# Token lists of all expert blocks built once by indirect 4-byte stores; gathers and weight loads four blocks ahead

## The chip, the cores and the metric

The kernel runs on one core of a Trainium2 chip. The metric is the device time of one launch in microseconds (us): 3921.82 us before, the median of three runs (3912.93, 3921.82 and 3946.88). TensorE (PE) multiplies matrices, and its weight loads are shown apart (PEld); VectorE is DVE, ScalarE is ACT, GpSimd is POOL and SyncE is SP. SP issues the plain loads on one DMA queue, POOL issues plain and indirect transfers on another; 16 DMA engines serve both.

## The reference, cut to what matters

Two layers of a diffusion backbone. Each mixes tokens (attention, pooling, windowed attention) and then runs a mixture of experts (MoE) over 768 tokens in layer 0 (256 context tokens and 512 latent ones) and over the 512 latent tokens in layer 1. A token chooses 8 of 64 experts. Each expert's tokens are padded to blocks of 128:

```python
idx = lax.top_k(sel, TOP_K)[1]                      # 8 experts of each token
order = jnp.argsort(flat_e)                         # assignments sorted by expert
dest = pad_start[sorted_e] + jnp.arange(A) - start[sorted_e]
row_tok = jnp.full((n_rows,), T, jnp.int32).at[dest].set(order // TOP_K)
...
def expert_block(args):                             # once per block of 128 rows
    tok, e = args
    xb = h_pad[tok]
    return (jax.nn.silu(xb @ w_eg[e]) * (xb @ w_eu[e])) @ w_ed[e]
...
routed = jnp.zeros((T + 1, D), h.dtype).at[row_tok].add(y * row_w[:, None])[:T]
return routed + shared                              # shared: one expert for all tokens
```

D_MODEL is 1024, an expert's hidden width 256, all of it in float32: the three weight matrices of a block are 1024 KB each. With the inputs of this case layer 0 has 76 blocks and layer 1 has 65, together 141.

## The kernel before, in words

All engines run programs written out by hand; a plan (`make_plan`, L74) lists jobs in one order that PE, ACT and DVE all follow, with three rotating PSUM slots: a job's PE part waits until the job three before it has been drained. Everything up to the MoE loop is such jobs. Those around the change, for each tile t of 128 tokens: `r` (router scores), `sg` (gate and up projection of the shared expert, L1000), `sT` and `sd` (transpose and down projection, L1005 and L1013), `pos` (each token's number within its expert, by triangular matmuls, L1020), then once `cnt`, `end`, `tab` (the table of blocks: expert, and place within the expert), and `first`.

`route` (L1320) is DVE's choice of 8 experts for a tile; POOL then stores the tile's weights into `h_rows` in DRAM (L1753), behind the token's row of 1024 floats. The outputs of the shared expert go to `acc` in DRAM, on POOL's queue (L1756, L1781).

**The expert loop** (`moe`) handles one block per step. PE's order in step n: gate and up matmuls of block n (L747, 16 records), eight transposes of the gathered rows of block n+1 (L719), `slots_of` (L734: one-hot times token numbers gives the token list of block n+2), the down matmuls of block n-1 (L783, 8 records), two transposes of the hidden rows of block n. DVE makes the one-hot (L1372), turns the product into indices (`take_index`, L1379 to L1384), halves the copies out of PSUM with ACT (L1389, L1430, L1401) and multiplies gate by up (L1396). POOL gathers rows with an indirect DMA (L1765) and adds results into `acc` with another (L1774; even and odd blocks go to two accumulators, and each store waits until the one of its accumulator two blocks before it has landed). The index of block n+2 is kept in one of four columns; before it is written, DVE waits for the store of block n-2, which uses that column. There are two buffers for gathered rows and two for weights (`WSL`, K and VY). SP loads gate and up of block n+2 when the gate and up matmuls of block n are done, and down of block n+1 when the down matmuls of block n-1 are done.

After the loop all engines meet, and `combine` adds the accumulators to the residual stream.

## Time and profile before

| what | value |
|---|---|
| median of the runs | 3921.82 us |
| the profiled execution's own time | 3961.87 us |
| its span, first to last instruction | 3960.0 us |
| mean granted PE clock | 0.930 of full speed |
| busy: PE, PEld, DVE, ACT, POOL | 91%, 56%, 30%, 19%, 13% |
| expert loop, layer 0 | from about 1218 to 2229 us |
| expert loop, layer 1 | from about 3059 to 3913 us |
| weight loads per block | 3 of 1024 KB |

The two expert loops are nearly half of the span. In a row of the timeline the columns are: start, duration, engine, line, operation, output and input tile, shapes, count; in brackets the idle time before it and what ended it. A row of the windows gives busy time of each engine with its number of instructions, then the granted clock, the busy share of the 16 DMA engines and the rate in GB/s.

### The profile page before, as it was taken

The page shows a single profiled execution, that of the slowest core. Times are in us where ns is not written, and L with a number is a line of the kernel's source. Part 1 is how long each engine was busy: PE and PEld are TensorE (multiplying, and loading weights), DVE is VectorE, ACT ScalarE, POOL GpSimd, SP SyncE. Part 2 cuts the span into 40 slices and gives each one's busy share as a digit, 9 for nine tenths or more (in the row PEclk, how much of TensorE's full clock was granted, in tenths as well). Part 3 has the DMA queues.
Part 4 walks back from the last instruction along what each step waited for, and adds up shares of the span by engine and source line. Part 5 has one row for each costly group of instructions (what it writes and reads, how often), then busy time and mean ns, then how long its engine had stood idle before and what let it go on. Part 6 is the DMA issues. An engine that isn't in the chain of part 4 may idle for free.

```text
span 3960.0 us, 45512 instructions
## 1 busy us (share of the span) xinstructions
PE 3595.2 (91%) x14248; PEld 2233.7 (56%) x14248; DVE 1173.0 (30%) x2319; ACT 756.3 (19%) x1339; POOL 518.1 (13%) x418
## 2 busy tenths in 40 slices
PE   7899999999998998999999499999998999999994
PEld 3479777799654444444444247876764444444442
DVE  2252222123242222222222425333323222222223
ACT  2342222121111111111111225232211111111111
POOL 0000300000001121222222300010000112122122
PEclk9999856999998999999999799979998999999997
DMA  6310100343327999999999720102323999999996
GB/s 225 97 33 27 62 22 16 113 148 114 128 87 259 305 294 293 296 317 301 309 318 297 227 79 1 46 17 64 96 98 146 301 302 293 304 309 302 294 300 187
DMA packets 221226, 735.22 MB, mean 186 GB/s; under 512 B 45573, under 2 KB 93863, under 8 KB 166980
## 3 DMA queue, kind: packets, MB, share of 16 engines
q1 hardware_dynamic: 174420, 596.12, 41.8%
q0 software_dynamic: 46704, 137.66, 15.3%
q8 instruction: 74, 1.21, 0.1%
q14 instruction: 28, 0.23, 0.0%
HBM read 671.68 MB, written 97.88 MB: 194 GB/s over the span
## 4 chain that ended last, share of the span: by engine, by line
PE 62%; DMA 26%; DVE 5%; issue 4%; ACT 1%; POOLq 1%; SPq 0%; DVEq 0%; POOL 0%; ACTq 0%
DMA acc<-region_q,idx 14%; DMA region_c<-h_rows,idx 12%; PE ps L783 8%; PE ps L719 7%; PE ps L690 6%; PE ps L890 6%; PE ps L697 5%; PE ps L699 5%; PE ps L698 5%; PE ps L909 5%; PE ps L747 5%; PE ps L983 3%; PE ps L1000 2%; PE ps L811 1%; DVE region_q L1430 1%
## 5 line engine op out<-in xcount | busy, mean ns | idle before, releaser
L719 PEld LDWEIGHTS ps<-con,region_c 128*128 128x128 f32 x2342 | 333.6, 183 | 390.3 <-DMA region_c<-h_rows,idx 202.1
L719 PE MATMUL ps<-con,region_c 128*128 128x128 f32 x2342 | 393.8, 305 | 167.5 <-DMA region_c<-h_rows,idx 141.2
L747 PE MATMUL ps<-region_k,region_q 128*128 128x512 f32 x1136 | 502.4, 595 | 1.7 <-DVE region_q L1389 1.7
L747 PE MATMUL ps<-region_v,region_q 128*128 128x512 f32 x1120 | 492.4, 592 | 0.8 <-DVE region_q L1389 0.8
L1050 ACT ACTIVATE region_q<-ps 128x512 f32<-128x512 f32 (+2 forms) x310 | 195.3, 630 | 837.0 <-PE ps L783 483.7
L747 PEld LDWEIGHTS ps<-region_k,region_q 128*128 128x128 f32 x1136 | 211.9, 192 | 241.7 <-issue 241.7
L747 PEld LDWEIGHTS ps<-region_v,region_q 128*128 128x128 f32 x1120 | 207.9, 191 | 235.4 <-issue 234.4
L1765 POOL DMA_INDIRECT region_c<-h_rows,idx x145 | 152.0, 1048 | 1301.6 <-DVE idx L1384 1104.9
L699 PE MATMUL ps<-region_x_split,ring_split 128*128 128x384 f32 (+2 forms) x800 | 284.9, 356 | 0.0
L783 PE MATMUL ps<-region_k,region_c 128*128 128x512 f32 x568 | 283.2, 644 | 1.0 <-DVE region_c L1401 1.0
L783 PE MATMUL ps<-region_v,region_c 128*128 128x512 f32 x560 | 273.7, 634 | 1.0 <-DVE region_c L1401 1.0
L1396 DVE SCALAR_TENSOR_TENSOR region_c<-region_c,ps 128x256 f32<-128x256 f32 x141 | 67.8, 481 | 688.4 <-ACT region_c L1066 688.4
L1774 POOL DMA_INDIRECT acc<-region_q,idx x141 | 238.9, 1694 | 198.1 <-DVE region_q L1430 150.9
L1066 ACT ACTIVATE region_c<-ps 128x256 f32<-128x256 f32 x141 | 54.2, 384 | 910.8 <-PE ps L747 910.8
L783 PEld LDWEIGHTS ps<-region_k,region_c 128*128 128x128 f32 x568 | 111.0, 206 | 116.2 <-issue 116.2
L783 PEld LDWEIGHTS ps<-region_v,region_c 128*128 128x128 f32 x560 | 107.6, 203 | 111.0 <-issue 111.0
L697 PE MATMUL ps<-region_x_split,region_q_split 128*128 128x384 f32 (+1 forms) x432 | 159.0, 368 | 7.5 <-DVE ring_split L1312 4.6
L1372 DVE TENSOR_TENSOR region_c<-con,posm 128x768 bf16 (+1 forms) x147 | 123.1, 837 | 125.7 <-issue 125.7
L699 PEld LDWEIGHTS ps<-region_x_split,ring_split 128*128 128x128 f32 x800 | 152.4, 190 | 12.0
L1430 DVE COPY region_q<-ps 128x512 f32<-128x512 f32 x141 | 97.5, 692 | 207.6 <-PE ps L783 206.8
L1389 DVE COPY region_q<-ps 128x512 f32<-128x512 f32 x143 | 98.3, 688 | 191.7 <-PE ps L719 191.7
L698 PE MATMUL ps<-region_h_split,region_q_split 128*128 128x384 f32 (+1 forms) x432 | 153.6, 355 | 0.0
(268 smaller groups left out, 4490.4 us busy)
## 6 DMA issues: line engine op xcount, KB each, us to landing
region_k<-in_w_exp_gate SPq DMA_DIRECT2D x71, 1024.0 KB
region_k<-in_w_exp_up SPq DMA_DIRECT2D x71, 1024.0 KB
region_k<-in_w_exp_down SPq DMA_DIRECT2D x71, 1024.0 KB, 7.8
region_v<-in_w_exp_gate SPq DMA_DIRECT2D x70, 1024.0 KB
region_v<-in_w_exp_up SPq DMA_DIRECT2D x70, 1024.0 KB
region_v<-in_w_exp_down SPq DMA_DIRECT2D x70, 1024.0 KB, 8.1
ring<-in_w_mod SPq DMA_DIRECT2D x24, 2048.0 KB, 8.0
ring<-in_w_in SPq DMA_DIRECT2D x26, 1024.0 KB, 5.7
```

The source lines that it names most:

```text
L690: last = mm(ps[0:rows, at:at + n], weight[k], src[k][:, tok:tok + n], start=k == 0, stop=k == len(weight) - 1)
L697: mm(o, wh, xh, start=k == 0, stop=False)
L698: mm(o, wh, xl, start=False, stop=False)
L699: last = mm(o, wl, xh, start=False, stop=k == len(stationary) - 1)
L719: last = nc.tensor.transpose(ps[0:t.shape[1], at:at + t.shape[0]], t, ident[0:t.shape[0], 0:t.shape[0]])
L747: last = mm(m_gu[s], xgT[:, s, k, :], wgu[s][:, :, k, :], start=k == 0, stop=k == DK - 1)
L783: last = mm(m_y[:, 512 * side:512 * side + 512], hTb[:, 1 - s, cc * P:cc * P + P], wdn[1 - s][:, cc, 512 * side:512 * side + 512], start=c ...
L890: last = mm(ps[:, at:at + n], q, k, start=True, stop=True)
L909: last = mm(OB[g % 2][:, VD * h:VD * h + VD], PTb[:, i % 2, j * P:j * P + P], v, start=j == 0, stop=j == len(ks) - 1)
L1050: return A_(o, i, ACT.Copy)
L1765: pool.indirect_dma_start(xg[:, s, :], None, H, bass.IndirectOffsetOnAxis(ap=idx[:, i4:i4 + 1], axis=0), bounds_check=TOK - 1, oob_is_err= ...
L1774: pool.indirect_dma_start(ACC[s], bass.IndirectOffsetOnAxis(ap=idx[:, i4:i4 + 1], axis=0), yb[:, s, :], None, compute_op=ALU.add).then_inc ...
```

## The change

The one-hot products, `take_index` and the `first` job are gone. Instead, `place_tokens` computes for each tile and each of its 8 choices one address in a list in DRAM (`slot_list`, 128 x 384 numbers, a column for every possible block of every expert), and POOL stores the token numbers there with 8 indirect DMAs of 128 x 4 bytes per tile: 48 in layer 0, 32 in layer 1. The lists were filled with numbers of dummy tokens at the start of the kernel. SP then loads the whole list back into SBUF once (192 KB), DVE shifts it right by 3 bits, and in the loop POOL copies the column of a block into a small index tile before each gather and each adding store.

`pos` of a tile now follows its `sg` job, so the routes and the placing alternate with the shared expert's work; the last two come after the last but one `sg`. The stores of the shared expert's results move from POOL's queue to SP's. There are four buffers of gathered rows (two of them in `region_h`) and four of weights (two of them in the ring of weight panels). SP loads block n+4 when block n is done; POOL gathers block n+3 in the step in which block n-1 is added.

```diff
-            if i == len(A) - 1:
-                for u in A:
-                    add("pos", l, u, drain="dve")
+            add("sg", l, t, drain="dve", panel=("shgu", l))
+            if i < len(A) - 1:
+                add("pos", l, t, drain="dve")
+            if i == len(A) - 2:
+                add("pos", l, A[-1], drain="dve")
                 add("cnt", l, drain="dve")
                 add("end", l, drain="dve")
                 add("tab", l, drain="dve")
-                add("first", l)
-            add("sg", l, t, drain="dve", panel=("shgu", l))
...
-        WSL = [K, VY]
+        WSL = [K, VY, ring[:, 0:6144], ring[:, 6144:12288]]
...
+                sp.wait_ge(sl["listed"], 16 * TOPK * len(A))
+                sp.dma_start(slots, LISTS[l].rearrange("(p n) a -> p (n a)", p=P)).then_inc(sl["list_in"], 16)
+                for n in (len(A) - 2, len(A) - 1):
+                    store_shared(n)
+                sp.wait_ge(filled, names["sd", l, A[-1]].fill)
+                for n in range(2, DEPTH_W):
+                    load_gate_up(expert(n), n)
+                    load_down(expert(n), n)
...
-                            with sp.If(n + 2 < n_blocks):
+                            with sp.If(n + DEPTH_W < n_blocks):
+                                e = expert(n + DEPTH_W)
                                 sp.wait_ge(sl["gu_done"], n + 1)
-                                load_gate_up(expert(n + 2), s)
-                            with sp.If(n + 1 < n_blocks):
-                                sp.wait_ge(sl["dn_done"], n)
-                                load_down(expert(n + 1), 1 - s)
+                                load_gate_up(e, r)
+                                sp.wait_ge(sl["dn_done"], n + 1)
+                                load_down(e, r)
...
-                                pe.wait_ge(sl["idx_ready"], n + 2)
-                                slots_of(r + 1, n + 3)
...
+            def place_tokens(l, t, ps):
+                ...
+                stt(base, ps[:, 0:E], float(LISTN), cst("listbase"), ALU.mult, ALU.add)
+                link(tt(past, ps[:, 0:E].unsqueeze(2).broadcast_to([P, E, MAXB - 1]), levels, ALU.is_gt))
+                vec.tensor_reduce(b, past, AX.X, ALU.add).then_inc(drained["dve"], 1)
+                dve.wait_ge(drained["dve"], names["pos", l, t].count)
+                link(stt(u, b, 1.0 - P * LISTN, base, ALU.mult, ALU.add))
+                link(tt(u, u, M, ALU.mult))
+                link(vec.max(best[:], u))
+                ts(place[:, 8 * n:8 * n + 8], best[:], -1.0, None, ALU.add).then_inc(placed, 1)
...
+                dve.wait_ge(sl["list_in"], 16)
+                ts(slots, slots, 3, None, ALU.logical_shift_right).then_inc(sl["slots_ready"], 1)
...
-                                dve.wait_ge(sl[f"scat{s}"], 16 * (UNROLL // 2 * m + (r + 1) // 2 + 1))
-                                take_index(n + 3, (r + 3) % 4)
...
                     pool.wait_ge(w_ready, n + 1 + (NT if l else 0))
                     pool.dma_start(H[t * P:t * P + P, D:HROW], Wt[:, n % 2, :]).then_inc(s_w[n % 2], 16)
+                    pool.wait_ge(placed, n + 1 + (NT if l else 0))
+                    for j in range(TOPK):
+                        at = bass.IndirectOffsetOnAxis(ap=place[:, 8 * n + j:8 * n + j + 1], axis=0)
+                        pool.indirect_dma_start(LISTS[l], at, choices[:, 8 * t + j:8 * t + j + 1], None)\
+                            .then_inc(sl["listed"], 16)
...
+                def gather(w, n, free=None):
+                    at = column(n)
+                    if free is not None:
+                        pool.wait_ge(sl["h_ready"], free)
+                    gp.tensor_copy(idx_in[:, w:w + 1], slots[:, bass.ds(at, 1)]).then_inc(sl["in_ready"], 1)
+                    pool.wait_ge(sl["in_ready"], n + 1)
                     pool.sem_inc(turns, 1)
-                    pool.indirect_dma_start(xg[:, s, :], None, H, bass.IndirectOffsetOnAxis(ap=idx[:, i4:i4 + 1], axis=0),
-                                           bounds_check=TOK - 1, oob_is_err=False).then_inc(sl[f"gat{s}"], 16)
...
+                def add_block(s, k, before):
+                    at = column(k)
+                    pool.wait_ge(sl[f"scat{s}"], 16 * (before + 1))
+                    gp.tensor_copy(idx_out[:, s:s + 1], slots[:, bass.ds(at, 1)]).then_inc(sl["out_ready"], 1)
+                    pool.wait_ge(sl["out_ready"], k + 1)
                     pool.wait_ge(sl["y_a"], k + 2)
                     pool.wait_ge(sl["y_b"], k + 2)
...
-                            with pool.If(n < n_blocks):
-                                pool.wait_ge(sl["h_ready"], n + 1)
-                                gather(s, (r + 3) % 4, n + 3)
+                            with pool.If(n + 3 < n_blocks):
+                                gather(r, n + 3, n)
```

## Rows read from the trace of the kernel before

**Rows 1.** Windows: the two expert loops, an undisturbed 48 us, and 5 us after a wait.
```profile
1218.00:2229.00 1011.00, 933.31 (x3040) 466.42 (x3040) 281.16 (x609) 120.04 (x229) 209.97 (x153) 0.96 0.92 296
3059.00:3913.00 854.00, 785.46 (x2470) 389.75 (x2470) 222.70 (x521) 102.45 (x196) 175.51 (x131) 0.97 0.92 293
...
2020.00:2068.00 48.00, 45.40 (x157) 22.59 (x156) 14.14 (x32) 6.32 (x12) 10.42 (x8) 1.00 1.01 335
...
1465.00:1470.00 5.00, 5.00 (x16) 2.64 (x15) 1.29 (x4) 0.60 (x1) 0.43 (x1) 0.50 0.73 305
```

**Rows 2.** One line's instructions (L747), then timelines at the loops' starts and ends.
```profile
L747 PE MATMUL ps<-region_k,region_q x1136: 592/592/1193, 1218.3 to 3902.4; 128*128 128x512 f32 x190
...
2228.42 0.69 DVE L1430 COPY region_q<-ps 128x512 f32<-128x512 f32 x1 [2.21 <-PE ps L783]
...
3059.26 7.11 PE L747 MATMUL ps<-region_k,region_q 128*128 128x512 f32 x16 [0.87 <-DVE region_q L1389]
...
3912.62 0.69 DVE L1430 COPY region_q<-ps 128x512 f32<-128x512 f32 x1 [2.28 <-PE ps L783]
```

**Rows 3.** Timeline of PE in layer 0's loop: a late step, then a prompt one.
```profile
1453.68 7.03 PE L747 MATMUL ps<-region_k,region_q 128*128 128x512 f32 x16
1463.90 1.97 PE L719 MATMUL ps<-con,region_c 128*128 128x128 f32 x8 [3.19 <-DMA region_c<-h_rows,idx]
...
1471.69 7.03 PE L747 MATMUL ps<-region_v,region_q 128*128 128x512 f32 x16
...
1479.45 0.29 PE L734 MATMUL ps<-tokb,region_c 128*128 128x3 bf16 x6
1479.60 3.68 PE L783 MATMUL ps<-region_k,region_c 128*128 128x512 f32 x8
...
1483.34 7.03 PE L747 MATMUL ps<-region_k,region_q 128*128 128x512 f32 x16
```

**Rows 4.** Waits of the whole span: total us, times, longest.
```profile
POOL region_c L1765 <- DVE idx L1384: 1104.9, 122, 12.3
...
PEld ps L719 <- DMA region_c<-h_rows,idx: 202.1, 75, 4.3
...
DVE pcol L1379 <- DMA acc<-region_q,idx: 169.8, 120, 3.0
```

**Rows 5.** Timeline in layer 0's loop: from an adding store to the gather behind it.
```profile
1702.20 2.32 POOL L1774 DMA_INDIRECT acc<-region_q,idx  x1 [0.30 <-issue]
...
1711.96 0.16 DVE L1379 COPY pcol<-ps 128x3 f32<-128x3 f32 x1 [0.98 <-DMA acc<-region_q,idx]
...
1713.48 1.04 POOL L1765 DMA_INDIRECT region_c<-h_rows,idx  x1 [8.96 <-DVE idx L1384]
...
1721.17 1.16 PE L719 MATMUL ps<-con,region_c 128*128 128x128 f32 x8 [0.15 <-DMA region_c<-h_rows,idx]
```

**Rows 6.** The adding stores (L1774), from issue to landing.
```profile
DMA to landing us min/median/max: 6.0/9.0/12.4
```

**Rows 7.** DMA issues, last figure us to landing: a 256 KB load, the expert-weight stores.
```profile
ring<-in_w_pool SPq DMA_DIRECT2D x2, 256.0 KB, 2.9
...
h_rows<-rt POOLq DMA_DIRECT2D x10, 32.0 KB, 1.7
```

**Rows 8.** Timeline ahead of the two loops, up to their first transposes.
```profile
1130.77 13.95 PE L1000 MATMUL ps<-ring,region_h 128*128 128x512 f32 x32
...
1138.47 0.54 POOL L1753 DMA_DIRECT2D h_rows<-rt  x1 [4.53 <-DVE rt L1357]
...
1183.32 0.19 PE L1020 MATMUL ps<-Mb,trib 128*128 128x64 bf16 x1
...
1216.24 1.16 PE L719 MATMUL ps<-con,region_c 128*128 128x128 f32 x8 [1.97 <-ACT region_q L1050]
...
2994.36 16.38 PE L1000 MATMUL ps<-ring,region_h 128*128 128x512 f32 x32
...
3057.24 1.15 PE L719 MATMUL ps<-con,region_c 128*128 128x128 f32 x8 [1.97 <-ACT region_q L1050]
```

More of the change, by code:

```diff
@@ L36 @@
 UNROLL = 4
+DEPTH_W = 4
+LISTN = E * MAXB
 HROW = D + E
@@ L44 @@
 _at = 0
-for _name, _n in (("ident", 128), ("ones", 128), ("perm16", 128), ("perm8", 128), ("tri", 128), ("tokid", 3 * NT), ("sel2", 2),
-                  ("thr", MAXB), ("iotan", TABN), ("dummy", 1), ("negdummy", 1), ("edges", 64), ("lower", 64),
-                  ("slot1", TOK)):
+for _name, _n in (("ident", 128), ("ones", 128), ("perm16", 128), ("perm8", 128), ("tri", 128), ("sel2", 2),
+                  ("thr", MAXB), ("iotan", TABN), ("edges", 64), ("lower", 64), ("listbase", E)):
     CONSTS[_name] = (_at, _at + _n)
@@ L262, in build @@
         scores = sb("scores", NT * E)
-        posm = sb("posm", NT * E)
+        key = sb("key", 3 * E)
+        over = sb("over", E * (MAXB - 1))
+        best = sb("best", 8)
+        place = sb("place", NT * 8, I32)
+        choices = sb("choices", NT * 8, I32)
         rt = sb("rt", 6 * E)
@@ L602, in _ @@
             for l in range(DEPTH):
+                sp.dma_start(LISTS[l].rearrange("(p n) a -> p (n a)", p=P), nobody).then_inc(s_empty, 16)
+            for l in range(DEPTH):
                 A = active(l)
@@ L620, in _, with store_shared @@
                 sl = L[l]
+                def store_shared(n):
+                    after(sp, "sd", l, A[n])
+                    sp.dma_start(ACC[0][A[n] * P:A[n] * P + P, :], yb[:, n % 2, :]).then_inc(s_sh[n % 2], 16)
                 sp.wait_ge(filled, names["o", l, A[-1]].fill)
+                for n in range(len(A) - 2):
+                    store_shared(n)
                 sp.wait_ge(tab_ready, l + 1)
@@ L722, in _, with moe @@
             tiles_done = [0]
-            def moe(l, part):
+            def moe(l):
                 sl = L[l]
@@ L746, in gate_up @@
                     for k in range(DK):
-                        last = mm(m_gu[s], xgT[:, s, k, :], wgu[s][:, :, k, :], start=k == 0, stop=k == DK - 1)
+                        last = mm(m_gu[s], xgT[:, s, k, :], wgu[w][:, :, k, :], start=k == 0, stop=k == DK - 1)
                     last.then_inc(sl["gu_done"], 1)
@@ L753, in turn_hidden @@
                     turn(m_h, [(cc * P, hv[:, cc, :]) for cc in range(2)]).then_inc(sl["hT_done"], 1)
-                if part == "first":
-                    slots_of(0, 1)
-                    pe.wait_ge(sl["idx_ready"], 1)
-                    slots_of(1, 2)
-                    return
                 turn_tokens(0, 16)
@@ L763, in moe @@
                 turn_tokens(1, 16)
-                slots_of(2, 3)
                 turn_hidden(0, 0)
@@ L1357, in route @@
                 ts(Wt[:, n % 2, :], t3, inv, ROUTED, ALU.mult, ALU.mult).then_inc(w_ready, 1)
-            def moe(l, part):
+            def place_tokens(l, t, ps):
+                M, (base, u, b) = Mb[:, t * E:t * E + E], (key[:, i * E:i * E + E] for i in range(3))
+                n = active(l).index(t)
+                a, _ = CONSTS["thr"]
+                levels = con[:, a + 1:a + MAXB].unsqueeze(1).broadcast_to([P, E, MAXB - 1])
+                past = over[:].rearrange("p (e k) -> p e k", e=E)
+                stt(base, ps[:, 0:E], float(LISTN), cst("listbase"), ALU.mult, ALU.add)
[6 more added lines that the diff above has]
+                ts(place[:, 8 * n:8 * n + 8], best[:], -1.0, None, ALU.add).then_inc(placed, 1)
@@ L1642, in _ @@
                     last = tt(hb[:, n % 2, :], s1[:, n % 2, :], ps[:, DE:2 * DE], ALU.mult)
-                    last.then_inc(drained["dve"], 1)
-                    last = None
-                    if n < 2:
-                        route(l, NT - 2 + n)
                 elif kind == "pos":
-                    t = a[1]
-                    last = tt(posm[:, t * E:t * E + E], ps[:, 0:E], Mb[:, t * E:t * E + E], ALU.mult)
+                    place_tokens(l, a[1], ps)
+                    n = active(l).index(a[1])
+                    if n + 2 < len(active(l)):
+                        route(l, active(l)[n + 2])
                 elif kind == "cnt":
@@ L1775, in add_block @@
                                             yb[:, s, :], None, compute_op=ALU.add).then_inc(sl[f"scat{s}"], 16)
-                for s in range(2):
-                    gather(s, s, s + 1)
-                for n in (len(A) - 2, len(A) - 1):
-                    after(pool, "sd", l, A[n])
-                    pool.dma_start(ACC[0][A[n] * P:A[n] * P + P, :], yb[:, n % 2, :]).then_inc(s_sh[n % 2], 16)
+                pool.wait_ge(sl["slots_ready"], 1)
+                for w in range(2):
+                    gather(w, w)
@@ L1782, in _ @@
+                pool.wait_ge(filled, names["sd", l, A[-1]].fill)
+                for w in range(2, UNROLL):
+                    gather(w, w)
                 for s in range(2):
```

148 lines of the change are left out of this document (55 added, 93 removed).

## The prediction

> **What bounds the kernel now.** I read the windows of the two expert loops first. They take 1011 and 854 us, and in both PE is busy 92% of the time, at 0.96 of its clock, with the DMA engines 92% busy at 296 and 293 GB/s [rows 1]. Nothing is idle enough to be ignored, so the bound must be read from single steps. The loops run from the first gate-and-up matmul at 1218.3 to the last copy's end at 2229.1, and from 3059.3 to 3913.3 [rows 2]: 1010.8 and 854.0 us, 1864.8 us for 76 and 65 blocks, a mean step of 13.23 us.
>
> PE's timeline shows that there is no typical step. From 1471.69 to 1483.34 one takes 11.65 us: the matmuls follow each other without a gap. The one before, from 1453.68, takes 18.01 us [rows 3]. After its gate-and-up matmuls PE waits 3.19 us for gathered rows, and after that pause its clock is granted at 0.50, the lower of its two levels (1.2 GHz), for the next 5 us [rows 1], so that the transposes take 1.97 us and the down matmuls are slow too. PE's weight loads wait for gathers 75 times, 202.1 us in all [rows 4]: about every second step is late. No comparable wait for weights is in the list.
>
> Why is the gather late? An adding store starts on POOL at 1702.20; DVE's `take_index` waits until it has landed, to 1711.96; the gather that it feeds is issued at 1713.48, and PE gets the rows at 1721.17 [rows 5]. So each gather stands behind the landing of a store four blocks older, because they share an index column. That is 19 us from store to rows, of which the step offers 18.5 (11.65 + 6.87 to the end of the next gate-and-up). DVE stands in that wait 120 times, POOL waits for the index 1104.9 us in total [rows 4]. The loop is held by this chain, with PE close behind and the DMA engines next.
>
> **What is removed.** (a) The chain goes: the lists exist before the loop. A gather in the new kernel is issued when block n-1 has been handed to its adding store and is used three blocks later; from the code, PE needs it some 19 us (one step and a gate-and-up part) after its issue even in steps of 11.65 us, against the 7.7 us of the one above [rows 5]. (b) PE loses `slots_of`, 0.15 us a step (the next matmul starts 0.15 us after its start at 1479.45 [rows 3]). So PE alone would need 11.5 us a step, 141 x 11.5 = 1621 us. (c) DVE loses one-hot, copy and index work; it is 28% busy in the loop [rows 1], so this pays nothing by itself.
>
> **What the loop then waits for.** The DMA engines carry 296 GB/s x 1011 us / 76 = 3.94 MB a block in layer 0 and 293 x 854 / 65 = 3.85 MB in layer 1, and the change leaves that as it is. At 11.5 us a step they would need 342 and 335 GB/s. Two readings bound what they can do. The best long stretch, four prompt steps, holds 335 GB/s at a share of 1.01 [rows 1]: 11.8 and 11.5 us a block. Taking instead the loop's share for real occupancy, 0.92 of 13.3 and 13.14 us gives 12.2 and 12.1 us. I take 12.0 us, nearer the second, because a 48 us stretch can live on weights that came early, the whole loop cannot: 141 x 12.0 = 1692 us, **-173 us**. Ends: 1621 (-243, PE alone) and 141 x 12.2 = 1720 (-145).
>
> The Trainium skill, "DMA: Bandwidth & Descriptors", section Specifications, puts the HBM limit of a core at about 358 GB/s. By that figure a block would take 11.0 us of transfers, PE would be the bound, and the loops would come to 1621 us. No stretch here holds such a rate for 48 us, so I let the row decide.
>
> Weights four ahead add no speed by themselves, as they are not late now; they only let DMA and PE drift apart by more.
>
> **What is added in the loop.** POOL gets two register loads and two copies of 128 x 1 a step. No row has them; from below zero, from above I allow 1 us each, 4 us on top of the 2.7 us of its two indirect issues (1.04 and 1.59 to 2.32 [rows 5]). POOL is then 7 us busy of 12, still covered. A new wait: `add_block` now stands on the landing of the store two blocks before it ahead of its copy, and the next gather is queued behind it on POOL. That landing takes 9.0 us, 12.4 at most [rows 6], two steps are 24 us, so it costs nothing while this cover lasts.
>
> **What is added ahead of the loops.** 80 indirect stores, each on POOL. The nearest row is a gather's issue, 1.04 us plus 0.3 of dispatch (1.34); the dearer one the adding store, 1.59 + 0.3 = 1.89 [rows 5]. A store without add is nearer the gather; I take 1.34. In layer 0 the first tile can be placed when `sg` of tile 0 is through: half of 13.95 after 1130.77 plus some 2.5 us for `pos` and placing, 1140 [rows 8]. From there POOL works through 48 x 1.34 + 6 x 0.84 (the weight stores) = 69 us, to about 1210; by the last two tiles alone, placed together near 1184, it would be 1184 + 16 x 1.34 = 1205. Then: the last store lands, 1.7 us [rows 7]; the list load of 192 KB, about 3 us like a 256 KB load [rows 7]; shift, register loads and copy, 2 us; gather, 1.04 issue and 7.2 landing beside 6 MB of weights [rows 5]. Sum 15 us: first rows at 1225, against 1216.24 now [rows 8]: +9 us. In layer 1, placing starts near 3004 (half of 16.38 after 2994.36, and pos [rows 8]), 32 x 1.34 + 3 gives 3050, rows at 3065 against 3057.24: +8. Together **+17 us**. At 1.89 the two are +35 and +26, **+61**. From below: PE no longer waits for the first lists between the `pos` jobs and the last `sg` (5 us), so if POOL keeps up each start is about 6 us earlier, **-12**.
>
> The Trainium skill says in the same page, section "Queues, rings and completion order", that the descriptors of one queue are taken in ring order on each engine. By that the list load, which SP issues behind two blocks of weights, waits for them; they are 6.3 MB from about 1190, 19 us at 335 GB/s, out by 1209 and so ahead of the list in any case. It matters only if POOL is faster than I think, and would cap the lower end at zero instead of -12.
>
> `place_tokens` and the route (5.07 us a tile [rows 8], placing some 2.5 by seven small operations) are 8 us of DVE in the 11.4 us that PE spends on a tile: nothing. The shared expert's stores on SP stand ahead of nothing that is due. The dummy lists (2 x 192 KB) and 24 KB of choices are loaded early, against 370 KB less of constants: nothing.
>
> **Sum.** -173 + 17 = -156 us. On the profiled execution's own 3961.9 that is 3806; on the median of 3921.8, which is 40 lower, 3766. Where those 40 us lie is not shown; if a part is gather waits that unprofiled runs don't have, the gain is a little smaller. **I say 3770.**
>
> **The rivals.**
> 1. PE becomes the bound, 11.5 us a step: -243 + 17 gives 3695. For it: the four prompt steps in a row at 335 GB/s. Against: the share is then already 1.01. 17%.
> 2. The DMA engines don't gain at all beyond their present mean and the start is dear: 12.4 us a step (1748, -117) and +61: 3866. For it: mixed stretches move fewer bytes. Against: the clean stretch. 16%.
> 3. The step stays where it is: gathers are still late, since POOL issues them in order behind an adding store that waits for y. Then +17: about 3939. Against: three blocks of lead. 6%.
> 4. Slower: the indirect transfers starve behind up to four blocks of weights. Place: the copy of y of block n waits for the landing of the store of n-2, so a step can't be shorter than (landing + 2.2)/2. It decides from a landing of 21.8 us and makes the kernel slower from 24.2. If three further blocks of weights, 9.4 MB, stood ahead, they alone would be 28 us; at a landing of 28 the step is 15.1 us, +264: about 4190. Against: with one to two blocks outstanding it is 9.0, never above 12.4 [rows 6]. The Trainium skill, same page and section, has each engine alternate between the queues packet by packet, which would double a landing at most, to 18 us: no cost. 8%.
>
> The forecast (11.7 to 12.3 us a step) has 53%.
>
> **The numbers.** Range 3690 to 3865: it takes in rival 1, the bound of +61 and most of rival 2. What a measurement can tell from no change is about 1%, 39 us. Faster by more: the forecast, rival 1 and nearly all of rival 2, 0.83. Within 1%: rival 3 and a rest, 0.08. Slower: 0.09.
>
> **What would show it.** Steps of 11.5 to 12.3 us; hardly a wait of L719 for `region_c<-h_rows`, short waits of L747 for weights instead if the DMA bound holds; a clock near 1.00 in the loop; DMA share 0.97 or more and 320 to 340 GB/s. The first transposes 9 us later than now in layer 0, and an issue of the small stores near 1.04 us. It is wrong if L1430 or L1050 wait for the adding store's landing, if POOL's busy time nears the step, or if the small stores take over 2 us each.

## The result, and the profile after

The kernel after takes **3712.2 us** (median of 4 runs, 3690.0 to 3785.4) against 3934.4 us for the kernel before (median of 4, 3912.9 to 3961.1): 0.941 of it, 95% interval 0.932 to 0.951. I had said 3770, range 3690 to 3865. The slowest of the four executions, 3785.4 us, was in a slower state; it counts in the median and not in the ratio. The profiled execution took 3699.5 us, its span 3697.7.

The page of the kernel after: busy time by engine, what the DMA engines moved in 40 slices of 92 us, and the chain that ended last.
```profile
PE 3436.1 (93%) x13496; PEld 2137.5 (58%) x13496; DVE 975.2 (26%) x1798; ACT 755.5 (20%) x1337; POOL 631.0 (17%) x767
...
GB/s 241 81 58 7 72 40 58 120 139 146 104 66 218 345 354 348 354 354 355 350 359 297 166 47 1 49 18 69 90 100 71 320 350 343 340 352 344 340 342 149
...
PE 90%; DVE 3%; DMA 2%; issue 1%; ACT 1%; POOL 1%; SPq 0%; another core or an unknown queue 0%; POOLq 0%; DVEq 0%; ACTq 0%
```
Nine tenths of the path is PE itself. The windows of the two loops and of 100 us inside the first (length; busy us and instructions of PE, PEld, DVE, ACT, POOL; granted clock, DMA share, GB/s), beside [rows 1]:
```profile
1178.00:2050.00 872.00, 869.77 (x2576) 431.84 (x2575) 159.18 (x303) 119.19 (x227) 226.43 (x295) 1.00 0.98 337
1600.00:1700.00 100.00, 100.00 (x301) 49.87 (x300) 18.83 (x36) 14.21 (x27) 27.63 (x36) 1.00 1.02 356
2903.00:3651.00 748.00, 745.21 (x2202) 369.91 (x2202) 136.45 (x260) 102.06 (x195) 192.22 (x251) 1.00 0.97 329
```
PE is busy for all but 2 us of 872, at full clock, and the DMA engines hold 356 GB/s for 100 us, where the stretch of before in [rows 1] has 335 for 48 us. By the first gate-and-up matmul and the last copy's end, as in [rows 2], the loops are 1177.7 to 2050.3 and 2903.3 to 3651.0: 872.6 and 747.7 us, 1620.3 in all against 1864.8, **-244.5 us**, and 11.48 and 11.50 us a step.

PE's timeline of one step, beside [rows 3]: no gap, no late gather.
```profile
1474.45 7.03 PE L765 MATMUL ps<-ring,region_q 128*128 128x512 f32 x16
1481.32 1.05 PE L743 MATMUL ps<-con,region_h 128*128 128x128 f32 x8
1482.21 3.60 PE L792 MATMUL ps<-region_v,region_c 128*128 128x512 f32 x8
1485.65 0.39 PE L743 MATMUL ps<-con,region_c 128*128 128x128 f32 x2
1485.87 7.03 PE L765 MATMUL ps<-ring,region_q 128*128 128x512 f32 x16
```
Waits of the whole span (total us, times, longest), beside [rows 4]:
```profile
POOL acc L1775 <- DVE region_q L1421: 1004.0, 134, 11.5
...
PE ps L743 <- DMA region_c<-h_rows,idx_in: 28.7, 2, 16.3
```
The 75 late gathers have become two, the first rows of each layer. POOL's 1004 us are its wait for y.

**Part of the difference is not the change.** In the stretch from 450 to 650 us, attention of layer 0, whose code is the same in both, the profiled execution of before had TensorE's clock granted at 0.55, the one of after at 0.97. A repeat of the kernel after (below) had 0.53. One window each of before, after and that repeat:
```profile
450.00:650.00 200.00, 197.47 (x719) 148.04 (x718) 53.85 (x136) 49.85 (x126) 11.63 (x12) 0.55 0.06 19
```
```profile
450.00:650.00 200.00, 190.27 (x1099) 147.24 (x1098) 70.00 (x164) 64.99 (x147) 16.97 (x19) 0.97 0.14 47
```
```profile
450.00:650.00 200.00, 196.93 (x696) 146.78 (x694) 52.55 (x135) 49.65 (x126) 14.51 (x18) 0.53 0.06 20
```
In the last column but two is the clock. With the stretch layer 0's router starts at 1120.1 (before) or 1134.4 (the repeat), without it at 1044.1. So the two profiles differ by 262 us, of which 76 lie there; 3961.9 against the repeat's 3776.9, both with it, gives **-185 us** at like clocks. Even there 14 us lie ahead of the router. They are clock too: run 1 below has the code of before up to the router and no low stretch, and its router starts at 1045.7, 1.6 us from the kernel after. So the change itself is nearer **-199 us**.

### The profile page after: what moved, and what is told of

Read it like the earlier page. It is cut to its first block, busy times and chain, and to the rows that moved or that the text cites. A ratio compares the mean times of both kernels' runs of the same rounds, so it can differ in the third digit from the quotient of the medians.

```text
span 3697.7 us, 42657 instructions
## 1 busy us (share of the span) xinstructions
PE 3436.1 (93%) x13496; PEld 2137.5 (58%) x13496; DVE 975.2 (26%) x1798; ACT 755.5 (20%) x1337; POOL 631.0 (17%) x767
## 4 chain that ended last, share of the span: by engine, by line
PE 90%; DVE 3%; DMA 2%; issue 1%; ACT 1%; POOL 1%; SPq 0%; another core or an unknown queue 0%; POOLq 0%; DVEq 0%; ACTq 0%
PE ps L765 26%; PE ps L792 13%; PE ps L743 8%; PE ps L714 7%; PE ps L721 5%; PE ps L722 5%; PE ps L723 5%; PE ps L899 5%; PE ps L918 4%; PE ps L992 4%; PE ps L820 1%; PE ps L1009 1%; POOL slot_list L1745 1%; PE ps L1004 1%; PE ps L876 1%
## 5 line engine op out<-in xcount | busy, mean ns | idle before, releaser
L765 PE MATMUL ps<-ring,region_q 128*128 128x512 f32 x1120 | 492.2, 592 | 0.0
L1775 POOL DMA_INDIRECT acc<-region_q,idx_out x141 | 226.3, 1605 | 1060.1 <-DVE region_q L1421 1004.0
L765 PEld LDWEIGHTS ps<-ring,region_q 128*128 128x128 f32 x1120 | 207.9, 191 | 234.4 <-issue 234.4
L743 PE MATMUL ps<-con,region_c 128*128 128x128 f32 x1766 | 281.0, 288 | 51.3 <-DMA region_c<-h_rows,idx_in 28.7
L765 PE MATMUL ps<-region_k,region_q 128*128 128x512 f32 x576 | 258.2, 602 | 1.7 <-DVE region_q L1389 1.7
L792 PE MATMUL ps<-ring,region_c 128*128 128x512 f32 x560 | 252.0, 593 | 1.0 <-DVE region_c L1401 1.0
L765 PE MATMUL ps<-region_v,region_q 128*128 128x512 f32 x560 | 246.3, 593 | 0.7 <-DVE region_q L1389 0.7
L765 PEld LDWEIGHTS ps<-region_k,region_q 128*128 128x128 f32 x576 | 108.8, 194 | 126.1 <-issue 126.1
L765 PEld LDWEIGHTS ps<-region_v,region_q 128*128 128x128 f32 x560 | 103.9, 191 | 118.2 <-issue 117.2
L792 PEld LDWEIGHTS ps<-ring,region_c 128*128 128x128 f32 x560 | 101.3, 191 | 102.6 <-issue 102.6
L992 PE MATMUL ps<-ring,region_k 128*128 128x512 f32 x320 | 138.7, 592 | 0.0
```

The source lines that it names most:

```text
L743: last = nc.tensor.transpose(ps[0:t.shape[1], at:at + t.shape[0]], t, ident[0:t.shape[0], 0:t.shape[0]])
L765: last = mm(m_gu[s], xgT[:, s, k, :], wgu[w][:, :, k, :], start=k == 0, stop=k == DK - 1)
L792: last = mm(m_y[:, 512 * side:512 * side + 512], hTb[:, 1 - s, cc * P:cc * P + P], wdn[before][:, cc, 512 * side:512 * side + 512], start= ...
L992: last = mm(ps[:, 512 * half:512 * half + 512], MG[:, k, t * P:t * P + P], w[:, k, :], start=k == 0, stop=k == DK - 1)
L1775: pool.indirect_dma_start(ACC[s], bass.IndirectOffsetOnAxis(ap=idx_out[:, s:s + 1], axis=0), yb[:, s, :], None, compute_op=ALU.add).then_i ...
```

## The experiments

"Start" below is the time from the first router matmul of a layer to the first gate-and-up matmul of its loop: 98.2 and 78.5 us before (layer 0, layer 1), 133.6 and 101.3 after. In layer 0 it also depends on the clock that the router got: with the router at the full clock, as before, the unchanged kernel after has 120.8 (run 11). Each run was timed against the kernel before on its own chip.

**1. Only the chain is cut, no lists.** The kernel before with eight index columns instead of four:
```
-UNROLL = 4
+UNROLL = 8
-        idx = sb("idx", 4, I32)
+        idx = sb("idx", 8, I32)
-                                dve.wait_ge(sl[f"scat{s}"], 16 * (UNROLL // 2 * m + (r + 1) // 2 + 1))
-                                take_index(n + 3, (r + 3) % 4)
+                                take_index(n + 3, (r + 3) % 8)
```


> The kernel before, with one thing changed: eight index columns instead of four (loop unrolled by eight), so that DVE need not wait for an adding store to land before it writes the next index. Gathers and weights keep their old depth. Theory A (the chain store landing -> index -> gather held the loop): the gather of block n+2 goes out when block n's hidden rows are read, 10 us before it is needed, against a landing of 7 to 8 us; the step falls from 13.2 to 11.7 to 12.0 us, the waits of PE for gathered rows from 202 us to under 40, the ratio to 0.94 to 0.955 (3690 to 3760 us). Theory B (gathers were late because of crowded DMA engines and shallow buffers): step 13.0 or more, ratio 0.985 to 1.0.

Measured: 3758.7 us, ratio 0.959 (0.943 to 0.974). Its loop of layer 0, and its waits:
```profile
1144.00:2078.00 934.00, 902.66 (x3040) 446.00 (x3040) 276.24 (x609) 120.03 (x229) 200.75 (x153) 1.00 0.98 320
```
```profile
PEld ps L719 <- DMA region_c<-h_rows,idx: 130.7, 111, 2.6
```
Steps of 12.29 and 12.11 us, loops of 1720.7: 144 of the 244 us come from the one wait for the store's landing, read from [rows 5]. The gathers are still late, by a little: 111 times, 1.2 us on the mean. So theory A has the cause, but its step of 11.7 to 12.0 us and its waits under 40 us were too good. The other 100 us came only with the lists, which take the index work out from between DVE, PE and POOL. That is by elimination, since neither depth alone is worth much (runs 2 and 3); the lists with both depths at two were not run.

**2 and 3. Depth.** The kernel after with two weight buffers instead of four, and with two buffers of gathered rows instead of four (the gather of block n+2 goes out when block n is hidden):
```
-        WSL = [K, VY, ring[:, 0:6144], ring[:, 6144:12288]]
+        WSL = [K, VY]
```


> The changed kernel with two weight buffers instead of four, loaded at the times of the kernel before. Theory A (depth of the weights adds nothing): step 11.5 us as with four, ratio to the kernel before 0.935 to 0.95. Theory B (the deeper queue is what lets the DMA engines carry 350 GB/s): step 12.0 us or more, PE waits at the gate-and-up matmuls for weights, rate at most 335 GB/s, ratio 0.96 or more.

```
-                            with pool.If(n + 3 < n_blocks):
-                                gather(r, n + 3, n)
+                            with pool.If(n + 2 < n_blocks):
+                                gather(s, n + 2, n + 1, (r + 3) % 4)
```


> The changed kernel with two buffers of gathered rows instead of four: the gather of block n+2 goes out when block n's hidden rows have been read, as early as the kernel before could have. Lists and four weight buffers stay. Theory A (the lists alone pay): about 10 us from issue to need; step 11.5 to 11.7 us if a landing takes 8 us, ratio 0.935 to 0.95. Theory B (beside weights queued four deep a landing takes longer than 10 us, so the lead is needed): PE waits 1 to 3 us for rows in many steps, step 12.5 to 13.5, ratio 0.97 to 1.0.

Measured: 3740.0 us (0.950, 0.935 to 0.965), steps 11.56 and 11.66; and 3708.0 us (0.946, 0.930 to 0.961), steps 11.50 and 11.51. Going four deep with weights is worth 0.1 us a step, some 16 us; with rows, about nothing (loops of 1622.2 against 1620.3). Once the lists exist, a gather has time enough from two buffers.

**4. How much the DMA engines carry.** Half of the down matmuls are left out (of each block only half of the output columns are computed), so that PE asks for weights faster:
```
-                                for side in range(2):
+                                for side in range(1):
```


> The changed kernel without the down matmuls of the second half of the output columns (4 of 8 records a step; all transfers stay). PE then needs 9.8 us a step. By the prediction's term (the DMA engines need 12.0 us a block) the step could not fall below 11.5 at all. If 350 GB/s at a share of 1.02 is their limit, the step is 11.0 to 11.2 us (3.9 MB at 352 GB/s) and PE waits for weights; if they still had room, it falls towards 9.8 us at up to 400 GB/s.

Measured: one run, 3687.8 us. Windows of layer 0's loop, of 100 us of it and of layer 1's loop, and the waits:
```profile
1168.50:2013.30 844.80, 770.21 (x2272) 384.21 (x2272) 159.41 (x303) 119.30 (x227) 226.63 (x295) 0.97 0.99 349
...
1650.00:1750.00 100.00, 93.42 (x281) 46.95 (x280) 20.03 (x38) 15.13 (x29) 27.66 (x36) 0.97 1.02 363
...
2889.10:3638.60 749.50, 694.29 (x2032) 345.67 (x2032) 142.58 (x271) 106.67 (x203) 201.57 (x263) 0.96 0.98 342
```
```profile
PE ps L765 <- DMA ring<-in_w_exp_up: 63.9, 40, 3.2
PE ps L765 <- DMA region_k<-in_w_exp_up: 33.1, 18, 3.2
```
Now PE does wait for weights, and the step of layer 0 stops at 11.12 us, though its matmuls alone need 9.8: that is about the transfers' own bound, 0.4 us under PE's. Layer 1 has 68 blocks here and not 65, because the halved sums of layer 0 change what its tokens choose. Its loop of 749.5 us is then 11.02 a step, at 342 GB/s. My 12.0 us a block was not the DMA engines' limit.

**5. The start doubled.** Every small store is done twice, the second to a list that nobody reads:
```
                             .then_inc(sl["listed"], 16)
+                    for j in range(TOPK):
+                        at = bass.IndirectOffsetOnAxis(ap=place[:, 8 * n + j:8 * n + j + 1], axis=0)
+                        pool.indirect_dma_start(SPARE[l], at, choices[:, 8 * t + j:8 * t + j + 1], None)\
+                            .then_inc(sl["listed"], 16)
```


> The kernel after with every small store done twice: behind a tile's 8 stores of 4 bytes a token stand 8 more of the same, to a second list that nobody reads, and the list load waits for all 160. It measures what a small store costs where it stands. At 1.26 us each (0.96 busy and 0.30 between) 48 more are 60 us of POOL in layer 0 and 32 more 40 us in layer 1. Theory A (POOL's stores are the path that sets the start of the loops only at the last two tiles, whose lists are made together): only the 16 added ones of these and what POOL falls behind before count, 20 to 45 us in layer 0 and 20 to 35 in layer 1, 40 to 80 us for the kernel. Theory B (POOL works through the stores without a pause, as my prediction had it): all 80 count, +100 us. Theory C (the stores are covered and the start waits for weights and the list's load): under +20 us. The loops keep 11.5 us a step in all three. If PE's and DVE's jobs ahead of the loops wait longer for each other too, the small stores disturb them (delays of 5 to 7 us that the kernel after shows at 1100 and 2850).

Measured: 3884.7 us (3816.1 to 3891.3). Starts 199.4 and 149.4: 65.8 and 48.1 us more, 113.9 in all, for 80 x 1.26 = 101 us of POOL. Theory B: POOL's stores are the path, from the first list to the last, and nearly every one counts. Not quite all of the burst is stores: in the kernel after POOL also waits 4.20 and 4.56 us for the placing of a tile in layer 0 and 4.07 in layer 1, and 8.52 in layer 0 here. Of the 13 us above the 101, 5.5 are the list, which lands 10.6 and 13.9 us after its issue against 8.9 and 10.1. The next two are the longest waits of PE in layer 0 and 1 without a release:
```profile
PE ps L1023 <- issue: 18.0, 1, 18.0
...
PE ps L1037 <- issue: 24.6, 1, 24.6
```

**6. The same number of plain stores.** The added ones are without indices:
```
+                    for j in range(TOPK):
+                        at = (8 * n + j) * P
+                        pool.dma_start(SPARE[l][at:at + P, :], choices[:, 8 * t + j:8 * t + j + 1]).then_inc(sl["listed"], 16)
```


> As the kernel with every small store doubled, but the added 8 a tile are plain stores of 4 bytes from each of 128 partitions, issued by POOL: the same number of packets of the same size, without indices. It asks what delays the other engines while POOL stores (DVE's chained operations 1.2 us apart instead of 0.26, a wait of PE of 18.0 us that no release explains). A plain store of Wt takes POOL 0.58 us, so 80 added ones are about 0.6 + 0.3 each, 70 us of POOL. Theory A (the 4-byte packets and their completions delay the others): the same delays, and the start longer by 70 to 80 us in all. Theory B (the making of indexed descriptors on POOL delays them): only POOL's own 70 us and no more delays than in the kernel after; +50 to +70 us. The loops stay at 11.5 us a step in both.

Measured: 3760.5 us (3739.8 to 3824.9); starts 152.4 and 126.4 against 120.8 and 101.6 of the control beside it (run 11), 56.4 us more for 80 x 0.55 = 44 us of POOL, as theory B had it. PE's unexplained waits in the starts are 1.8 and 5.8 us, against 4.6 and 8.8 in the control, so more packets of 4 bytes do not make them longer. But here DVE waits up to 14.5 us for the weight store (`Wt` has two buffers, and the store stands behind the small ones on POOL), and it does so too in run 5 (7.5 and 8.0 us): part of what looks like disturbance there is this wait. In both runs the starts grow by POOL's added time plus 12 to 13 us.

**7. The list on POOL's queue.** In the kernel after SP issues the list load behind two blocks of weights; here POOL does:
```
-                sp.wait_ge(sl["listed"], 16 * TOPK * len(A))
-                sp.dma_start(slots, LISTS[l].rearrange("(p n) a -> p (n a)", p=P)).then_inc(sl["list_in"], 16)
+                pool.wait_ge(sl["listed"], 16 * TOPK * len(A))
+                pool.dma_start(slots, LISTS[l].rearrange("(p n) a -> p (n a)", p=P)).then_inc(sl["list_in"], 16)
                 pool.wait_ge(sl["slots_ready"], 1)
```


> The kernel after, with one edit: the list of slots is loaded by an issue on POOL's queue, right after the last small store has landed, instead of by SP, which issues it behind two blocks of weights and has its packets served behind them. In the kernel after the last small store of layer 0 is issued at 1148.67, the list load only at 1154.89, and it lands at 1163.8, when the weights ahead of it are in. Theory A (the list stands in SP's queue, not in the small stores): the list is there some 3 to 9 us sooner, so PE's wait for the first rows goes from 16.33 us to about 8 in layer 0 and from 12.36 to about 6 in layer 1: 10 to 18 us less for the kernel, loops unchanged at 11.5 us a step. Rival B (the weights' packets hold whatever shares the engines with them, from whichever queue): the list lands as late as before, 0 us. Rival C (the gathers then stand beside the weights and land later by what the list gained): the list is sooner, the first rows are not, 0 to -4 us.

Measured: 3685.8 us (0.943, 0.932 to 0.955), starts 119.2 and 96.8, with the router of layer 0 at full clock (10.8 us) as in the control: 1.6 and 4.8 us less than that. Under the 10 to 18 of theory A: the list lands 6.3 and 7.5 us after its issue, where the control has 8.8 and 9.5, but beside the weights it is not quick.

**8 and 9. Weights of blocks 2 and 3 held** until the rows of blocks 0 and 1 are in, on top of 7, run twice:
```
                 sp.wait_ge(filled, names["sd", l, A[-1]].fill)
+                for w in range(2):
+                    sp.wait_ge(sl[f"gat{w}"], 16)
                 for n in range(2, DEPTH_W):
```


> The same as the list on POOL's queue, and SP loads the weights of blocks 2 and 3 only when the rows of blocks 0 and 1 have landed. If the first gathers (7.7 to 9 us from issue to rows) are slow because of the 6.3 MB of weights beside them, PE's wait for the first rows loses another 3 to 5 us in each layer; if they are slow by themselves or for blocks 0 and 1's weights, nothing more. The price: blocks 2 and 3 then load while the loop runs, which at 342 GB/s has only some 10 GB/s to spare, so waits for weights may show in the first steps; 1 to 5 us a layer. Sum: -14 to -24 us against the kernel after if both hold, -5 to -12 if the held weights cost what they give.

> The list of slots loaded from POOL's queue and the weights of blocks 2 and 3 held until the rows of blocks 0 and 1 have landed, once more, this time beside the kernel after: its first profile had the starts shorter by 8.2 and 10.3 us with equal loops. If that is real, 15 to 20 us less than the kernel after (0.995 of it); if the two profiles differed by chance, within 5 us of it.

Measured: 3681.1 (0.945, 0.939 to 0.951) and 3691.8 us (0.942, 0.935 to 0.949). Starts 125.4 and 91.0, then 128.2 and 92.6, against 133.6 and 101.3 with layer 0's router at the lower clock in all three: 18.5 and 14.1 us less. The first rows in the first of them (compare the start of the kernel after in the next section):
```profile
1146.61 0.96 POOL L1745 DMA_INDIRECT slot_list<-choices,place  x1 [0.30 <-issue]
...
1152.55 0.59 POOL L1779 DMA_DIRECT2D region_c<-slot_list  x1 [4.97 <-DMA slot_list<-choices,place]
1159.22 0.36 DVE L1404 TENSOR_SCALAR region_c<-region_c 128x384 int32<-128x384 int32 x1 [12.90 <-DMA region_c<-slot_list]
...
1166.48 1.97 PE L743 MATMUL ps<-con,region_c 128*128 128x128 f32 x8 [11.44 <-DMA region_c<-h_rows,idx_in]
```
From the last small store to the rows it is 19.9 us, and 26.2 in the kernel after. In layer 0 the rows come 4.5 us after their gather's issue, against 8.8 with the weights of blocks 2 and 3 beside them. The steps stay at 11.47 to 11.51, so the held weights cost nothing.

**10. Block 1's weights held too**, until the list is in:
```
                 for n in range(2):
+                    if n:
+                        sp.wait_ge(sl["list_in"], 16)
```


> The same, and SP loads block 1's weights only when the list has landed. In the former the list load stood on POOL's queue at 1152.55 and its shift followed near 1160, beside the weights of blocks 0 and 1. If those 3.1 MB of block 1 are what slows it, list and first rows come 3 to 5 us sooner in each layer and block 1's weights (9 us at 345 GB/s) are still in before its gate-up matmuls at 10.4 us after the loop's start: 6 to 10 us less in all. If the list load is slow by itself, or block 1's weights come late, nothing or up to 5 us more.

Measured: 3691.3 us (0.941, 0.932 to 0.950); starts 126.3 and 94.9, no gain over runs 8 and 9. The first rows:
```profile
1157.37 0.59 POOL L1781 DMA_DIRECT2D region_c<-slot_list  x1 [4.66 <-DMA slot_list<-choices,place]
1160.08 0.36 DVE L1406 TENSOR_SCALAR region_c<-region_c 128x384 int32<-128x384 int32 x1 [8.72 <-DMA region_c<-slot_list]
1160.79 0.33 SPq L645 DMA_DIRECT2D region_v<-in_w_exp_gate  x1
...
1162.28 1.07 POOL L1765 DMA_INDIRECT region_c<-h_rows,idx_in  x1 [0.91 <-POOL idx_in L1762]
...
1172.05 1.97 PE L745 MATMUL ps<-con,region_c 128*128 128x128 f32 x8 [10.53 <-DMA region_c<-h_rows,idx_in]
```
The sum hides two effects. The list now lands in 2.7 us in both layers, against 6.3 to 7.5 beside block 1's weights (runs 7 and 9). But those weights go out as it lands, and the rows then take 9.8 us instead of 4.5. So the weights beside them are what makes the list and the rows slow, and holding them only moves the cost.

**11. The control**, the kernel after unchanged:

> The kernel after, unchanged, on the same chip and between the same rounds as the three variants beside it: a control. Expected: 3690 to 3715 us, loops at 11.48 to 11.50 us a step. It also shows how much the part ahead of the loops varies with nothing changed: from the first router matmul to the first gate-up matmul it took 133.6 us in layer 0 and 101.3 in layer 1; the router of layer 0 ran at the lower clock level there (20.1 us for its matmuls) and at the higher in other variants that share the code up to that point (10.5 us). If that is chance and not code, this run may show either, with the start 0 or 9.5 us shorter.

Measured: 3777.9 us (3775.2 to 3819.9), ratio 0.969 (0.958 to 0.979). Loops 872.5 and 747.5. It missed the expected 3690 to 3715 by 63 us, all of it ahead of layer 0's router (1134.4 against 1044.1). Its router had the full clock (10.8 us, not 20.6), and its starts are 120.8 and 101.6.

**12. The shared expert's stores back on POOL**, on top of 8:
```
+                    if 0 < n < len(A) - 1:
+                        after(pool, "sd", l, A[n - 1])
+                        pool.dma_start(ACC[0][A[n - 1] * P:A[n - 1] * P + P, :], yb[:, (n - 1) % 2, :])\
+                            .then_inc(s_sh[(n - 1) % 2], 16)
```


> On top of the list load on POOL's queue and the held weights of blocks 2 and 3, one more part of the change undone: the shared expert's rows are stored by POOL again, as before (each behind the small stores of the next tile), and not by SP. In every profile of the new kernel DVE's chain of small operations runs evenly while POOL makes its small stores (route takes 4.84 to 4.96 us against 4.70 without them) until SP issues its first store of shared rows (1087.41 in layer 0 of the kernel after, 1154.86 and 1162.74 in two variants, 2838.51 in layer 1); within 1.2 us of that DVE's operations stand 0.45 to 1.2 us apart, and route takes 6.4 to 22 us; PE, ACT and DVE then have waits of 2 to 18 us with no release shown. Theory A (the two together, SP's stores to the sums beside POOL's indexed stores, delay the others): route stays under 5.0 us for every tile, those waits go, and the starts are 5 to 15 us shorter in layer 0 and 3 to 8 in layer 1 than the 125.4 to 128.2 and 91.0 to 92.6 us of the two profiles without this edit, the kernel 3670 to 3680 us. Theory B (POOL's small stores alone do it, the coincidence is chance or comes from the amount outstanding): the stretched chains stay, and POOL's added 6 x 0.84 us make the starts 0 to 5 us longer.

Measured: 3677.4 us (3671.5 to 3751.5), the lowest median of all; its starts are 123.3 and 89.4, 2 to 5 and 2 to 3 us shorter. But `route` of the fourth tile still takes 6.25 and 5.73 us against 4.70. Theory A falls: SP's stores and the stretched chains only coincided. What the stores on SP do is hold the weights: here the first weights go out 92.0 us after the router's start, in the kernel after 100.1 us, where SP first waits for the fourth tile's rows. With the weights 8 us earlier the list lands in 2.8 and 2.7 us and the rows in 4.5.

## Why the prediction was right, and where it was not

The sign, the cause and the range held. What was named as forecast did not happen; **rival 1, PE becomes the bound, is what happened** in the loops, and the start was dearer than both said. At like clocks the change is -185 us, and the forecast was -156 on the profiled execution's own time: 72 us too little gain in the loops, 29 too little cost at the starts, and 14 us of clock ahead of them. That the number came so near is in part luck, as the two misses have opposite signs.

**The bound of before: right.** The wait for the store's landing in an index column used by four blocks carried the loop; run 1 takes it away by itself and gets 144 us.

**PE alone, 11.5 us a step: right** (11.48 and 11.50; 1621 us said, 1620.3 measured).

**The DMA term, 12.0 us a block: wrong, the largest miss.** I read a share of 1.01 at 335 GB/s [rows 1] as a limit. It was a demand. The kernel before has shorter stretches above it, which [rows 1] leaves out, one of them in its first loop:
```profile
1320.00:1340.00 20.00, 18.31 (x58) 8.86 (x57) 6.33 (x14) 2.18 (x4) 5.27 (x4) 1.00 1.00 354
```
With the queues never empty the same engines show 356 GB/s at a share of 1.02, and 363 when PE asks for more (run 4). A block costs them 11.1 us in layer 0 and 11.0 in layer 1. The share does not grow with what is carried, once it is near 1; so -173 should have been -243. The Trainium skill, "DMA: Bandwidth & Descriptors", section Specifications, gives about 358 GB/s for a core's HBM, and its sum, 11.0 us of transfers and PE as the bound, stood in the prediction as the way not taken. By its number these runs agree, with 356 to 363 GB/s in six windows of 100 us of run 4's loop, but as a limit they do not: the first window has 375, and finer slices go far over it. The DMA view of the kernel after, 1600 to 1700 us in slices of 2.5 us:
```profile
DMA  9999999999999999999999999999999999999999
GB/s 394 367 351 313 295 386 381 315 308 382 440 390 300 353 394 384 300 303 361 412 377 297 322 413 379 323 305 364 425 421 308 318 367 360 331 301 331 419 423 323
```
At an unchanged share the rate swings between 300 and 440. With weights of 1 MB a load in the queues beside adding stores and gathers of rows, 356 is the mean of a mix; which traffic makes the low slices was not tried.

**The start, +17 us: too small.** It is +22.6 and +23.1 by the control. The burst of small stores was well priced: 1.34 us said, 0.96 + 0.30 = 1.26 measured; 71.5 us from the first to the last in layer 0, 70 said. In those 71.5 us POOL also waits 8.8 for the placing. The step that failed is the tail from the end of the last store's issue to the first rows: 15 us said, 25.2 and 26.4 measured, 25.0 and 26.7 in the control. That is 22 of the 29 us. Another 6 come from the bursts, which end 3 us later than said in each layer of the control, and 1.6 from the first transposes, 1.97 us each at the lower clock after the pause instead of 1.16. Timeline of the kernel after (POOL, SP's queue, DVE, PE), beside [rows 8]:
```profile
1148.67 0.96 POOL L1745 DMA_INDIRECT slot_list<-choices,place  x1 [0.30 <-issue]
...
1153.70 0.33 SPq L650 DMA_DIRECT2D region_v<-in_w_exp_down  x1
1154.89 0.33 SPq L661 DMA_DIRECT2D region_c<-slot_list  x1
...
1163.80 0.36 DVE L1404 TENSOR_SCALAR region_c<-region_c 128x384 int32<-128x384 int32 x1 [16.42 <-DMA region_c<-slot_list]
1164.91 0.18 POOL L1760 COPY idx_in<-region_c 128x1 int32 x1 [15.28 <-DVE region_c L1404]
...
1166.01 1.08 POOL L1763 DMA_INDIRECT region_c<-h_rows,idx_in  x1 [0.92 <-POOL idx_in L1760]
...
1174.84 1.97 PE L743 MATMUL ps<-con,region_c 128*128 128x128 f32 x8 [16.33 <-DMA region_c<-h_rows,idx_in]
```
Between the last store and the list's issue 5.3 us pass, not 1.7: SP is still issuing weights until 1153.7, and even where POOL issues the load at once the last store is not landed for 4.9 us (run 7). In layer 1 of run 8, where no weights are out yet, that wait is 1.5 us. The list then takes 8.9 us (10.1 in layer 1), not 3, beside and behind 6.3 MB of weights. I had the weights through before the list would be asked for, since I let them start at 1190 with the list at 1210. In fact they go out between 1144.14 and 1153.70, just ahead of it. In the control they start 89 us after the router, before the change 70.5. Half of the delay is the table of blocks, written 9 us later. The other half is the fourth tile's shared rows, for which SP now waits first; the prediction said that these stores "stand ahead of nothing that is due".

The Trainium skill, same page, section "Queues, rings and completion order", has the descriptors of one queue taken in ring order; I said that it would not bind. On POOL's own queue beside the same weights the load takes 6.3 to 7.5 us, so the order behind the weights is worth 2 to 3 us. With the weights out of the way it takes 2.7 (runs 10 and 12), as said. So sharing the engines with them is worth the other 4 to 5.

**The rest around them.** With like clocks the span differs by -184.9: loops -244.8, starts +22.6 and +23.1, from loop 0's end to router 1 -0.1, after the loops 0.0, and +14.3 ahead of layer 0's router. In that last part the control's clock is a little lower still (0.75 against 0.82 in 400 to 500 us, 0.61 against 0.69 in 600 to 700): it is clock and not change. Run 1's router agrees (1045.7, against 1044.1 in the kernel after), so the change without it is -199.

**The 40 us** by which the profiled execution of before lay above the median of its runs: I could not place them. The times of the kernel before follow its mean granted clock (3893.7 us at 0.948 and 3994.2 at 0.921, beside run 11), so they look like clock; that they lie in attention's low stretch is not shown, since the other executions have no trace. No run shows a part of them in the gathers, as I had allowed.

**Rivals 3 and 4** did not come. POOL is 226 us busy of 872, and no gather is late after the first; run 3 shows that even two buffers don't bring back the wait.

**The new operations on POOL** (bounded at 1 us each): copies of 0.18 to 0.77 us, and 0.85 to 1.0 between the copy and the gather's issue. Covered, as said. **The `Wt` buffers** I had not seen at all: a ring of two whose store stands behind eight small stores on POOL. It just holds in the kernel after, and breaks when POOL has more to do (runs 5 and 6).

## What to carry to other kernels

A DMA share near 1 says that the queues hold work, not that the engines are full: before you price a transfer-bound step, find the stretches with the highest rate, short ones too, and take them as a lower bound on the capacity. Cutting a loop's chain is worth what the next resource allows, and here the plain fix (more index columns) had 144 of the 244 us. Work moved out of a loop is paid at the loop's door: follow it in order through each queue (the store's landing, the issue behind other issues, the load behind other loads), since every piece there is in series with PE standing idle.

## What the runs showed of the hardware that I had not expected

While POOL issues its indexed stores, small operations of other engines are delayed, though the stores' packets take only 2 to 3% of the DMA engines' time. DVE's `route`, a chain of short dependent operations, takes 4.70 us without them, up to its reciprocal. With them it takes 4.84 to 4.96 for most tiles, but 6.4 for the fourth tile in layer 0 and 7.3 in layer 1, 12.8 once in run 8 and 22.5 once in run 5. It begins 10 to 11 us after the first store in the five starts that I followed (1077.2 and 1087.2 in layer 0 of the kernel after). The kernel after, DVE in layer 0:
```profile
1088.67 0.23 DVE L1356 MAX8 rsm<-rt 128x8 f32<-128x64 f32 x1 [0.43 <-DVE rt L1355]
1089.43 0.22 DVE L1358 TENSOR_TENSOR rt<-rt 128x64 f32<-128x64 f32 x1 [0.20 <-DVE rt L1357]
1090.15 0.20 DVE L1359 CAST Mb<-rt 128x64 bf16<-128x64 f32 x1 [0.50 <-DVE rt L1358]
```
Each waits 0.2 to 0.5 us for the one before it on its own engine, where a few us earlier there is no gap. By run 6 more 4-byte packets do not make PE's waits longer, and by run 12 SP's stores do not stretch the chains. What does it stays open.

Layer 0's router ran at 20.6 us in some profiles and at 10.8 in others of the same code (its weight loads take 333 or 190 ns). The router alone is 9.8 us longer with the former and the whole start 12.8 (133.6 against 120.8), which is more than several of the edits tried here; only starts with the same router may be compared.
